# Layer normalisations by token halves: the last output tile and the first two chunks of the next stage are multiplied for the latent tokens and the context separately

## The reference, cut to what matters

```
def layer_norm(x):                       # over the 1024 channels of a token
    return (x - mean(x)) * rsqrt(var(x) + EPS)
def modulate(x, shift, scale):  return x * (1.0 + scale) + shift
def post_norm(x, y):            return layer_norm(ALPHA * x + y)
def swiglu(h, w_in, w_out):
    gate, up = split(h @ w_in, 2);  return (silu(gate) * up) @ w_out
```

## Time and profile before

| | |
|---|---|
| median of 3 runs | 2345.96 us (2343.65 to 2347.18) |
| profiled execution, its own time | 2342.77 us |
| its span, first to last instruction | 2340.9 us |
| PE busy | 2205.5 us, 94% of the span |
| DVE busy | 1421.8 us, 61% |
| ACT busy | 981.2 us, 42% |
| POOL busy | 751.5 us, 32% |
| mean granted PE clock | 0.975 |

### The profile page before, as it was taken

How to read it: one execution, slowest core, us unless ns; L and a number is a source line. 1 busy time by engine, 2 the same in 40 slices (tenths; PEclk the granted TensorE clock), 3 DMA queues, 4 the chain that set the end, 5 groups by cost and what they waited for, 6 DMA issues and landing times.

```text
span 2340.9 us, 33704 instructions
## 1 busy us (share of the span) xinstructions
PE 2205.5 (94%) x12994; PEld 1901.1 (81%) x12994; DVE 1421.8 (61%) x2103; ACT 981.2 (42%) x1587; POOL 751.5 (32%) x378
## 2 busy tenths in 40 slices
PE   6988989999999988989899999989999989988997
PEld 6977889988888876866688888878888868878997
DVE  3644454538887667757777766579656464446335
ACT  4655446543222335455442222253222254455443
POOL 3433325442222233421233322334222224214443
PEclk9999999999999998999999999999999999998999
DMA  7426535445464331110334443234454362213553
GB/s 259 164 91 260 227 128 189 158 176 197 165 223 184 125 106 56 55 64 1 126 108 149 166 171 121 96 135 156 170 205 148 105 144 91 73 52 131 178 185 105
DMA packets 79404, 329.94 MB, mean 141 GB/s; under 512 B 18912, under 2 KB 29280, under 8 KB 55696
## 3 DMA queue, kind: packets, MB, share of 16 engines
q1 hardware_dynamic: 79248, 327.81, 39.9%
HBM read 326.70 MB, written 1.08 MB: 140 GB/s over the span
## 4 chain that ended last, share of the span: by engine, by line
PE 82%; DVE 7%; issue 5%; ACT 5%; POOL 1%; DMA 0%; DVEq 0%; SPq 0%; ACTq 0%; POOLq 0%
PE ps L526 25%; PE ps L527 25%; PE ps L528 25%; ACT WH L986 1%; PE ps L669 1%; PE ps L700 1%; PE ps L660 1%; POOL WL L2120 1%; DVE WL L1491 1%; DVE TMP L1567 1%; PE ps L645 1%; PE ps L679 1%; DVE AR L1904 0%; DVE X L1750 0%; DVE TMP L1594 0%
## 5 line engine op out<-in xcount | busy, mean ns | idle before, releaser
L2120 POOL TENSOR_TENSOR WL<-WF,WH 128x1024 fp32r<-128x1024 f32 (+2 forms) x253 | 593.8, 2347 | 1359.5 <-ACT WH L986 1359.0
L526 PE MATMUL ps<-Hh,WH 128*128 128x512 f32 (+1 forms) x2504 | 859.2, 343 | 61.9 <-DVE Hl L1738 28.9
L527 PE MATMUL ps<-Hl,WH 128*128 128x512 f32 (+1 forms) x2504 | 853.2, 341 | 0.0
L528 PE MATMUL ps<-Hh,WL 128*128 128x512 f32 (+1 forms) x2504 | 852.5, 340 | 0.0
L986 ACT CAST WH<-WF 128x1024 fp32r<-128x1024 f32 (+3 forms) x507 | 467.5, 959 | 321.6 <-PE ps L528 310.8
L526 PEld LDWEIGHTS ps<-Hh,WH 128*128 128x128 f32 x2504 | 481.2, 192 | 129.1 <-issue 73.7
L528 PEld LDWEIGHTS ps<-Hh,WL 128*128 128x128 f32 x2504 | 480.8, 192 | 52.0
L527 PEld LDWEIGHTS ps<-Hl,WH 128*128 128x128 f32 x2504 | 481.4, 192 | 51.0 <-issue 0.2
L1567 DVE CUSTOM_DVE_ANT_0 TMP<-AR 128x1024 f32<-128x1024 f32 x216 | 416.1, 1966 | 9.8 <-DMA AR<-in_ada 8.9
L1491 DVE TENSOR_TENSOR WL<-WF,WH 128x1024 fp32r<-128x1024 f32 (+2 forms) x254 | 314.1, 1237 | 147.6 <-ACT WH L986 147.0
L526 PE MATMUL ps<-HIDh,WH 128*128 128x512 f32 (+1 forms) x880 | 307.0, 349 | 3.8 <-DVE WL L1491 3.8
(11 more groups left out here) (225 smaller groups left out, 2067.2 us busy)
## 6 DMA issues: line engine op xcount, KB each, us to landing
WF<-in_w SPq DMA_DIRECT2D x170, 1024.0 KB, 4.9
AR<-in_ada SPq DMA_DIRECT2D x120, 512.0 KB, 5.7
WF<-in_w SPq DMA_DIRECT2D x80, 704.0 KB, 4.1
AR<-in_piece SPq DMA_DIRECT2D x12, 1024.0 KB, 8.5
AR<-bias_rows SPq DMA_DIRECT2D x3, 1024.0 KB, 13.6
AR<-in_rpb SPq DMA_DIRECT2D x12, 256.0 KB, 6.6
AR<-in_cond SPq DMA_DIRECT2D x2, 1024.0 KB, 7.0
X<-in_x SPq DMA_DIRECT2D x2, 512.0 KB, 4.2
```

The lines of the kernel that those rows point to most:

```text
L526: e.matmul(out, lh, rh, start=first, stop=False)
L527: e.matmul(out, lh, rl, start=False, stop=False)
L528: return e.matmul(out, ll, rh, start=False, stop=end)
L2120: e.tensor_tensor(l[:, k0:k1, :], src[:, k0:k1, :], h[:, k0:k1, :].bitcast(F32), ALU.subtract).then_inc(*up("p_lo", ("lo", i, 1)))
```

## The change

Three things are changed.

1. **The last output tile** of every stage from f10 on (`pe_last`) is multiplied first for the latent columns and then for the context columns. The averages over partitions are taken for 256 tokens at a time (`pe_mean_begin`, `pe_mean_end`). Those of the latent half stand inside the context half of the tile; those of the context half end inside the next stage. In the last two norms, where there are only 256 tokens, `pe_mean_begin` stands ahead of the tile's last k.
2. **The first two chunks after a norm** (`pe_joint`) are multiplied for the latent tokens through all k, and then for the context. ACT (`act_norm`) and DVE (`dve_norm_halves`) work in the same order, on 256 columns at a time. The split of the second of these chunks, which stood before and inside the norm, is now among the first tiles after it.
3. **In f10** the two chunks are multiplied for the context first, which was made ready long before, and the average of the final norm of the first block is taken inside. Of chunk 0 only, then of chunk 1, then the latent half of both.

```
+    def pe_joint(e, before, T, of, *chunks):
+        step = pe_begin(e, of, *chunks)
+        step(0, 0, 0)
+        if T > S:
+            pe_mean_end(e, before, 1)
+        step(0, 1, 0)
+        step(1, 0, 0)
+        step(1, 1, 0)
+        for k in range(2, KT):
+            step(0, k, 0)
+            step(1, k, 0)
+        for r in range(1, T // S):
+            for k in range(KT):
+                for x, (_, tokens, _) in enumerate(chunks):
+                    if tokens > S:
+                        step(x, k, r)
+    def pe_last(e, i, st, T, of, c0):
...
+        for r in range(T // S):
...
+            b = ps.take(e, (st, "d7", r), (st, "x7", r))
+            for k in range(n):
...
+                if r == 1 and k == 1:
+                    pe_mean_begin(e, st, 0)
+                if r == 1 and k == 3:
+                    pe_mean_end(e, st, 0)
+                if r == T // S - 1 and k == n - 2:
+                    pe_mean_begin(e, st, r)
+    def act_norm(e, before, st, l, g, T):
+        i, two = AFTER[before], T > S
+        act_square7(e, before, 0)
+        act_mean(e, before, 0)
+        act_deviation(e, before, 0)
         e.wait_ge(*at(("mod", l, g)))
         for k in range(KT):
...
+            act_modulate(e, st, l, g, k, 0)
+            if k == 1 and two:
+                act_square7(e, before, 1)
+            if k == 2 and two:
+                act_mean(e, before, 1)
+            if k in (1, 2):
+                act_half(e, i, k - 1)
+            if k == 3 and two:
+                act_deviation(e, before, 1)
+        if two:
+            for k in range(KT):
+                act_modulate(e, st, l, g, k, 1)
         e.mul(SQ[:, 0:T], STAT[0][:, 0:T], ALPHA).then_inc(*up("mean", (before, "up")))
+    def dve_norm_halves(e, before, gate, st, l, g, T):
+        two = T > S
+        dve_gated7(e, before, *gate, 0)
+        dve_variance(e, before, 0)
+        dve_centre(e, before, 0, 0)
+        dve_centre(e, before, 1, 0)
         e.wait_ge(*at(("mod", l, g)))
...
+        dve_modulate(e, st, before, l, g, 0, 0)
+        dve_modulate(e, st, before, l, g, 1, 0)
+        dve_modulated(e, st, l, g, 0, 0)
+        if two:
+            dve_gated7(e, before, *gate, 1)
+        for k in range(2, KT):
+            if k == 3:
+                dve_split(e, AFTER[before])
+            dve_modulated(e, st, l, g, k - 1, 0)
+            dve_centre(e, before, k, 0)
+            dve_modulate(e, st, before, l, g, k, 0)
+            if k == 4 and two:
+                dve_variance(e, before, 1)
+        dve_modulated(e, st, l, g, KT - 1, 0)
+        if two:
+            for k in range(KT + 1):
+                if k < KT:
+                    dve_centre(e, before, k, 1)
+                    dve_modulate(e, st, before, l, g, k, 1)
                 if k:
...
+                    dve_modulated(e, st, l, g, k - 1, 1)
```

More of the change, by code:

```diff
@@ L521, in acts, with pe_product, pe_lin @@
         return [(*of[k], [(n, k) for n in events]) for k in range(len(of))]
[L525 to L530, removed]
+    def pe_product(e, out, lh, ll, rh, rl, first, end, parts=False):
+        e.matmul(out, lh, rh, start=first, stop=False, skip_group_check=parts)
+        e.matmul(out, lh, rl, start=False, stop=False, skip_group_check=parts)
+        return e.matmul(out, ll, rh, start=False, stop=end, skip_group_check=parts)
+    def pe_lin(e, i, of, T, tiles, fresh=False, mid=None, wide=2, part=False):
         h, l = parts_of(i)
@@ L557, in pe_lin, with pe_begin @@
                             mid()
-    def pe_pair(e, of, *chunks):
-        outs = [[ps.take(e, t, *freed) for t, freed in tiles] for _, _, tiles in chunks]
+    def pe_begin(e, of, *chunks):
+        outs = [[None] * len(tiles) for _, _, tiles in chunks]
         n = nk(chunks[0][0])
         kc = (n + 1) // 2
[L564 to L580, removed]
@@ new lines, in pe_begin, with step @@
+        order = []
+        def step(x, k, r):
+            i, T, tiles = chunks[x]
+            h, l = parts_of(i)
+            hi, lo, ready = of[r][k]
+            c = slice(S * r, S * r + S)
+            first = (x, k) not in order
+            over = order.count((x, k)) == T // S - 1
+            order.append((x, k))
+            if k == 0 and first:
+                outs[x] = [ps.take(e, t, *freed) for t, freed in tiles]
+            if k in (0, kc) and first:
+                e.wait_ge(*at(("hi", i, int(k >= kc))))
+                e.wait_ge(*at(("lo", i, int(k >= kc))))
+            if x == 0:
+                for y in ready:
+                    e.wait_ge(*at(y))
+            for j, (t, _) in enumerate(tiles):
+                col = slice(P * j, P * j + P)
+                m = pe_product(e, outs[x][j][:, c], h[:, k, col], l[:, k, col], hi[:, c], lo[:, c], k == 0, k == n - 1, True)
+                if over and k == n - 1:
+                    m.then_inc(*up("tile", ("done", t), *([("end", i)] if j == len(tiles) - 1 else [])))
+                elif over and k == kc - 1 and j == len(tiles) - 1:
+                    m.then_inc(*up("half", ("half", i)))
@@ new lines, in pe_swiglu @@
+    def pe_swiglu(e, st, before, T):
+        of = acts(hf)
+        pair = [(CH[st + "_gu"][n], T, gate_tiles(st, n)) for n in range(2)]
+        for h in range(2):
+            if h == 0 and st == "f10":
+                step = pe_begin(e, [acts(hf, "f10h", "f10l"), acts(hf, "cxl")], *pair)
+                for k in range(KT):
+                    step(0, k, 1)
+                    if k == 1:
+                        pe_stat(e, "final", S, [(HT[4], ("fsum", 5)), (HT[10], ("fsq", 6)), (HT[11], ("fsq", 7))])
+                for k in range(KT):
+                    step(1, k, 1)
+                for k in range(KT):
+                    step(0, k, 0)
+                    step(1, k, 0)
+            elif h == 0:
+                pe_joint(e, before, T, normed(st, T // S), *pair)
@@ L860, in one_gla @@
             some(1)
[L862 to L863 removed]
+        pe_joint(e, "f10", T2, normed("mix0", 2), (CH["e_q"][0], T2, [(("gq", j), [("gq", j)]) for j in range(2)]),
+                 (CH["e_lr"][0], T2, [(("lr", 0), [("lrt",), ("krrot",), ("krc",)])]))
         def gates():
```

308 lines of the change are left out of this document (157 added, 151 removed).

## The result

| | before | after |
|---|---|---|
| median, runs on one chip | 2346.57 us (2343.65 to 2347.38, 4 runs) | 2375.11 us (2373.68 to 2380.23, 4 runs) |
| profiled execution | 2342.77 us | 2373.68 us |
| its span | 2340.9 us | 2371.9 us |
| PE busy | 2205.5 us | 2220.1 us |
| mean granted clock | 0.975 | 0.977 |

The change makes the kernel slower: ratio 1.0128, 95% interval 1.011 to 1.0146, +28.5 us between the medians. The prediction was 2367 us in a range of 2350 to 2380, slower with 0.87. The time lies in the range, in the case that was called likeliest, though at its upper edge of 2376; the forecast loss of 21 us was 8 us too small.

The account below looks back on a forecast made before the run. PE, busy 94% of the span, was taken as the bound. Changes by norm sum to +15.8 us, with POOL +4 and clock +1 to +20.8: 2363.6 profiled, 2367 as median (3.2 above profiled before), range 2350 to 2380.

Parts of the forecast that it names:

- The restart: Norm into f11: PE restarts 12.0 us after the last tile's start instead of 17.15, idle only 1.5, no lower clock.
- The latent half at the pitch of the hand-over: Latent half after a norm: DVE, ACT and DVE in turn take 1.97 us per tile, where PE needs 1.44.
- The rival "faster": Latent half: a tile takes DVE 1.44 us or less, so PE never waits after restarting; -26 us, 2320; chance 0.09.
- The second pair of loads, the hole at tile 4: Context root inside the latent half: extra Ln and Exp table loads delay tile 4, so PE waits 2.5 us.
- POOL's share of the split: In the norms: POOL's half of the split beside DVE's steps slows DVE; +4 us, bounds 0 to 12.
- The end: Last norm: two means precede the last 3 steps (+0.8), one more centring behind the root (+0.4); +1.2 us.
- f11: Norm into f11: PE starts the third chunk 42.25 us after the last tile's start, for 41.35 before; +0.9 us.
- f20: Norm into f20: condition's silu and a table load before the third chunk's split, and late sums; +7.0 us.
- mix0: Norm into mix0: `e_lr` is half as wide, so PE has 1.08 us of work against DVE's 1.97; +4.3 us.
- mix1: Norm into mix1: context half is one chunk, and `n_v` needs both halves, its half 1 starting late; +4.4 us.
- f21: Norm into f21, 256 tokens: variance 1.5 us later, 1.97 per tile for 1.44, third chunk behind silu load; +4.9 us.
- f10: Start of f10: context steps fill PE's wait from 495.32 to 502.40 and avoid the lower clock; -6.9 us.

Follow-up runs that it names:

- e2: Changed kernel with DVE centring and scaling tile k before it makes `Hl` of tile k-1 in the latent loop: 2360.32 us.
- e5: One table set for both ln and exp in place of the ln set: 2357.39 us on the changed kernel, 2330.17 us on the kernel before.
- e4: Changed kernel with POOL's share of the second chunk's split in each norm cut from 1024 to 8 columns: 2363.35 us.
- e3: Changed kernel with tile 4 of the sums collected after output tile 6 again, not after tile 5, on ACT and DVE: 2371.97 us.

## Why the prediction was right, and where it was short

- **The restart**: right. 12.0 us behind the last tile's start, after an idle of 1.32, at full clock.
- **The latent half at the pitch of the hand-over**: right, 1.92 for 1.97, shown by e2: with ACT covered, the pitch is 1.25 and 13 us of the loss go by the stages. The rival "faster" needed a pitch of 1.44 and had its middle at 1.65; the measured 1.92 lies above both.
- **The second pair of loads, the hole at tile 4**: the hole is there (2.72 of wait, forecast 2.5). One load of the two is on the path, as e5 shows; the variance behind tile 4's scaling covers the other.
- **POOL's share of the split** (+4): the mechanism was right and the size less than half. The step took one neighbouring row, 1.3 lost, and a lesser share of it in two norms. The loss is 2.0 to 2.1 in four norms and 0.4 in mix0, all of it on PE's path: 8.8 (e4).
- **The sum's missing term**: the prediction cost the early collection of tile 4 at nothing. Tile 4's sum and square were added behind output tile 5 and no longer behind tile 6, an edit of the changed kernel that its description in three points doesn't name. The prediction said of the sums and the split only that they are done "about 5.1" behind the tile's start, and never asked what now stands ahead of the last tile's own weights on DVE. That is 1.36, 1.40, 1.36 and 1.85 us of PE in the norms into mix0, f11 and mix1 and at the end. e3 takes all four away, and with the clock at the end 7.9 us.
- **The end** (+1.2 for +4.9): 1.85 is that wait, about 1.5 the clock of 0.52 behind it, which no step had at the end.
- **f11** (+0.9 for +4.7), **f20** (+7.0 for +9.5), **mix0** (+4.3 for +5.6), **mix1** (+4.4 for +7.1): each is near its step plus the terms just named, with 4.5, 9.1, 6.2 and 8.0.
- **f21** (+4.9 for +3.6, with POOL's 2.0 in the 3.6): this step was 3.3 too large. The sums were ready sooner than before, as the wait of 3.27 in place of 4.29 shows, and the restart came 8.8 us behind the start of the means for 8.4, +0.4 where the step had the variance 1.5 later.
- **f10** (-6.9 for -6.0): right. PE waits 1.02 for the third chunk, which the step had not.
- **The clock** (+1): not settled. It can't be told from the spread, as one fall more or less is worth 1.5 us or more, and the fall that is seen at the end was in no step.
- **Table drains**: no room for them in the rows, as said. In e5 on after each load taken off the path between the variance and the restart gave 1.28, the load's own time.
- **The number**: the stages behind the first line give +29.4 for 20.8. The collection makes 7.9 of it and POOL 4.8, and f21 takes 3.3 back. So it was partly luck that the time stayed within 8 us of the forecast: two errors of one sign met one of the other.

## What to carry to other kernels

A dependent chain that crosses engines once per tile is bound by the round trip, not by the busy time, unless the list puts the next tile's work between the two ends; skew the order first, then split a norm. When work is moved earlier to free a later step, look at what stood behind it in the queue: here two sums moved ahead of the last tile's weights cost more than they gave. And before rebuilding the order around five waits of 6 us, look at what they are made of: the table load of 1.28 between Ln and Exp went with one word, and with what it moved elsewhere gave 15 us by the medians, where the rebuilding lost 28.
